# A block's attention units taken from tiles 0 and 3 in turn, then from tiles 1 and 2, and six products without use left out

## The reference

```python
def causal_attention(q, k, v):
    def one_block(args):          # a block is Q_BLOCK = 128 queries
        qb, bi = args
        scores = jnp.einsum('bqhd,bkhd->bhqk', qb, k) * scale
        q_pos = bi * Q_BLOCK + jnp.arange(Q_BLOCK)
        scores = jnp.where(k_pos[None, :] <= q_pos[:, None], scores, -jnp.inf)
        probs = jax.nn.softmax(scores, axis=-1).astype(v.dtype)
        return jnp.einsum('bhqk,bkhd->bqhd', probs, v)
...
    o = causal_attention(q, k, v)
    return rms_norm(o.reshape(b, s, MLA_OUT), out_g)
```

## Time and profile before

| | us |
|---|---|
| median of 3 runs | 2030.34 |
| lowest, highest | 2025.52, 2040.3 |
| the profiled execution's own time | 2028.29 |
| its span | 2026.7 |
| busy in it: PE, DVE, ACT, POOL | 1886.3, 1577.2, 1214.2, 449.5 |
| the block's first product on PE, the next block's | 579.13, 644.42 |

### The profile page before, as it was taken

One profiled execution on the slowest core, in us unless ns is written; L12 is line 12 of the kernel. 1 busy time (PEld: TensorE's weight loads), 2 busy tenths in 40 slices (PEclk: granted clock), 3 DMA queues, 4 the chain that ended last, 5 costly groups with the idle time before them and its releaser, 6 DMA issues.

```text
span 2026.7 us, 27081 instructions
## 1 busy us (share of the span) xinstructions
PE 1886.3 (93%) x9331; PEld 1503.6 (74%) x9331; DVE 1577.2 (78%) x1614; ACT 1214.2 (60%) x1246; POOL 449.5 (22%) x381
## 2 busy tenths in 40 slices
PE   7989988787999886899999999999999999999997
PEld 5766655675767674788888888888888888888884
DVE  4763353674456566889999999999999999999996
ACT  5544564423455322257777777777777777777773
POOL 3435543001034242061311111111111111111110
PEclk9999998998999898799999999999999999999998
DMA  7535441505101105499999999999999999999994
GB/s 201 165 101 190 135 141 44 184 9 134 54 1 28 26 2 179 160 305 348 398 389 398 390 398 389 398 388 390 392 388 394 386 393 381 396 388 394 389 370 148
DMA packets 180401, 525.06 MB, mean 259 GB/s; under 512 B 34530, under 2 KB 52018, under 8 KB 180338
## 3 DMA queue, kind: packets, MB, share of 16 engines
q1 hardware_dynamic: 156882, 458.27, 59.7%
q0 software_dynamic: 21376, 65.95, 11.2%
q10 hardware_dynamic: 2080, 0.01, 0.1%
HBM read 499.06 MB, written 25.12 MB: 259 GB/s over the span
## 4 chain that ended last, share of the span: by engine, by line
PE 56%; DVE 2%; issue 0%; POOLq 0%; POOL 0%; DVEq 0%
PE banks L3354 52%; PE banks L3342 3%; PE banks L3348 1%; PE banks L3418 0%; DVE expert_weights L3692 0%; DVE x_tokens L3688 0%; DVE weights_lo L3488 0%; DVE x_tokens L3699 0%; DVE x_tokens L3571 0%; PE banks L3475 0%; PE banks L3439 0%; PE banks L3409 0%; DVE u_lo L3524 0%; DVE rows_lo L3518 0%; DVE member L3551 0%
## 5 line engine op out<-in xcount | busy, mean ns | idle before, releaser
L3488 DVE TENSOR_TENSOR weights_lo<-expert_weights,weights_hi 128x2048 fp32r<-128x2048 f32 x384 | 877.0, 2288 | 67.3 <-ACT weights_hi L3728 64.2
L3728 ACT ACTIVATE weights_hi<-expert_weights 128x2048 fp32r<-128x2048 f32 x384 | 738.8, 1926 | 266.6 <-PE banks L3354 260.0
L3354 PE MATMUL banks<-weights_hi,rows_hi 128*128 128x512 f32 x1024 | 319.6, 393 | 0.0
L3354 PE MATMUL banks<-weights_hi,rows_lo 128*128 128x512 f32 x1024 | 315.9, 390 | 0.0
L3354 PE MATMUL banks<-weights_lo,rows_hi 128*128 128x512 f32 x1024 | 274.6, 390 | 0.0
L3354 PEld LDWEIGHTS banks<-weights_hi,rows_hi 128*128 128x128 f32 x1024 | 190.0, 188 | 45.1 <-issue 7.3
L3354 PEld LDWEIGHTS banks<-weights_hi,rows_lo 128*128 128x128 f32 x1024 | 192.5, 188 | 40.6
L3354 PEld LDWEIGHTS banks<-weights_lo,rows_hi 128*128 128x128 f32 x1024 | 192.8, 188 | 40.2
L3354 PE MATMUL banks<-weights_hi,u_hi 128*128 128x512 f32 x512 | 161.3, 396 | 1.4 <-DVE u_lo L3524 1.4
L3354 PE MATMUL banks<-weights_hi,u_lo 128*128 128x512 f32 x512 | 158.7, 391 | 0.0
L3354 PE MATMUL banks<-weights_lo,u_hi 128*128 128x512 f32 x512 | 137.5, 390 | 0.0
(11 more groups left out here) (592 smaller groups left out, 2756.6 us busy)
## 6 DMA issues: line engine op xcount, KB each, us to landing
expert_weights<-in_exp_w SPq DMA_DIRECT2D x384, 1024.0 KB, 9.4
enter_rows<-in_ada_w POOLq DMA_DIRECT2D x24, 1024.0 KB, 5.7
w_in_landing<-in_w_in SPq DMA_DIRECT2D x16, 384.0 KB, 3.2
second_landing<-in_w_in SPq DMA_DIRECT2D x12, 512.0 KB, 3.6
x_tokens<-in_x SPq DMA_DIRECT2D x8, 512.0 KB, 6.5
w_in_landing<-in_w_in SPq DMA_DIRECT2D x8, 512.0 KB, 3.7
enter_w_landing<-in_w_out SPq DMA_DIRECT2D x8, 512.0 KB, 5.3
leave_w_landing<-in_w_o SPq DMA_DIRECT2D x8, 512.0 KB, 10.0
```

The lines of the kernel that those rows point to most:

```text
L3354: last = nc.tensor.matmul(c.banks[:, bank + n, :], left[:, 2 * q + kk, :], right[:, q, kk * FF + n * 512:kk * FF + (n + 1) * 512], start=s ...
L3488: nc.vector.tensor_tensor(w_lo[:, ch % SPLIT, :], c.raw[:, ch % RAW if place is None else place, :], w_hi[:, ch % SPLIT, :], ALU.subtract) ...
L3728: nc.scalar.activation(w_hi[:, ch % SPLIT, :], c.raw[:, ch % RAW if place is None else place, :], ACT.Copy).then_inc(hi_ready.sem, 1)
```

## The change

The order of the tiles becomes `PAIRED = (0, TT - 1, 1, 2)`, that is 0, 3, 1, 2. Units 0 to 15 go through the heads and take tile 0 and tile 3 of each; units 16 to 31 do so with tiles 1 and 2. `place_of(i)` gives the place of a unit's tile in the order (0 or 1 in the first half, 2 or 3 in the second), which picks the output bank and the columns of the sums; `units_until(g)` gives the number of units after which the tile at place g is complete: 15, 16, 31, 32. The takes of the first two places stand after `hide` of units 19 and 20, the other two after the loop (before: after units 11, 19 and 27, and at the end). The six products without use inside the loop are gone; those behind it stay. The last tile is now tile 2, so the next block squares the rows of that one. The side work keeps its unit numbers.

```diff
+PAIRED = (0, TT - 1, 1, 2)
...
-    order = tuple(range(TT))
-    units = [(h, t) for t in order for h in range(NH)]
+    order = PAIRED
+    units = [(h, t) for pair in (order[0:2], order[2:4]) for h in range(NH) for t in pair]
+    place_of = lambda i: 2 * (i // (2 * NH)) + i % 2
+    units_until = lambda g: 2 * NH * (g // 2 + 1) - 1 + g % 2
...
-                    g = i // NH
+                    g = place_of(i)
                     if h == 0 and g >= 2:
 
                         pe.wait_ge(taken.sem, g - 1)
...
                     if i in (6, 7):
                         spread_inverses(i - 4)
-                    elif i < 10:
-                        nc.tensor.matmul(c.banks[:, 5, 0:256], c.ident[:], v_tok[:, 0, 0:256], start=True, stop=True)
...
-                                         accum_out=total[:, i:i + 1]).then_inc(probs.sem, 1)
+                                         accum_out=total[:, place_of(i) * NH + units[i][0]:place_of(i) * NH + units[i][0] + 1]).then_inc(probs.sem, 1)
...
-                    dve.wait_ge(probs.sem, (g + 1) * NH)
+                    dve.wait_ge(probs.sem, units_until(g))
...
-                    dve.wait_ge(out_ready.sem, (g + 1) * NH)
+                    dve.wait_ge(out_ready.sem, units_until(g))
...
-                    if i >= 11 and i % NH == 3:
-                        take(i // NH - 1)
+                    if i in (19, 20):
+                        take(i - 19)
+                take(TT - 2)
                 take(TT - 1)
...
-                last_rows = latent["rows"](TT - 1)
+                last_rows = latent["rows"](PAIRED[-1])
...
-                                                          accum_out=latent["sums"][:, TT - 1:TT]))
+                                                          accum_out=latent["sums"][:, PAIRED[-1]:PAIRED[-1] + 1]))
```

## The result

| | before | after |
|---|---|---|
| median of 20 runs each | 2030.42 | 2040.63 |
| lowest, highest | 2025.52, 2040.3 | 2033.01, 2046.43 |
| the profiled execution's own time, its span | 2028.29, 2026.7 | 2035.01, 2033.4 |
| the block's first product, the next block's | 579.13, 644.42 | 581.32, 654.88 |
| the block | 65.29 | 73.56 |

The account below looks back on a forecast made before the run. VectorE was taken to bound the block's start and middle, TensorE its end. Order -0.8 and clock +1.6 made +0.8 us on the median 2030.34, so 2031.1 us, range 2024 to 2037.

Parts of the forecast that it names:

- What bounds the kernel: In the block the change touches first, VectorE sets the start and middle, TensorE the end.
- the start: Up to TensorE's iteration 8: wide units delay unit 4 to 592.2, and TensorE reaches iteration 8 at 597.0.
- the middle: VectorE's masks and side work to the second take: 14.3 us plus 0.9 for waits, ending at 620.2.
- The end: TensorE's work after the second take: 191 steps, 20.9 us, plus 0.3 for the last copy; last output at 641.4.
- the order's term: Whole block: the new tile order alone moves the last output from 642.2 to 641.4, a gain of 0.8 us.
- The clock: Two TensorE stands in the middle, 2.8 and 1.9 us, halve its pace for 3.4 us at the end's beginning: +1.6.
- the one on the other side: At the end the clock stays down, 13 us as from 301 to 314: +5.7, to 2036.0 us; chance 0.13.
- the rival of 6.4 us gained: TensorE never waits in the middle, takes come in time: 2023.9 us; chance 0.12.
- that of +3: The middle is 2 to 3 us longer on VectorE, from last exponents or GpSimd contention: 2033.5 us; chance 0.10.
- The range: Whole time from 2024 to 2037 us, holding all cases, the upper end widened by one.

Follow-up runs that it names:

- fill_both: Changed kernel plus unused 512-column products where TensorE stood, three before unit 16's outputs and two before unit 17's: block 66.05 us.
- fill_bonus_early: fill_both with the copies of the head sums one iteration earlier: block 65.08 us.
- fill_second: Changed kernel plus two unused 512-column products in TensorE's second stand only, before unit 17's outputs: block 67.49 us.
- wake_dense: Changed kernel plus three unused 512-column products in TensorE's iteration 22, after the clock's fall: block 70.92 us.
- wake_thin: Changed kernel plus thirteen unused 64-column products in TensorE's iteration 22, after the clock's fall: block 78.02 us.
- fill_first: Changed kernel plus three unused 512-column products in TensorE's first stand only, before unit 16's outputs: block 71.05 us.
- takes_early: Changed kernel with the two middle takes moved to units 18 and 19, bonus products and scaled rates two units later: block 70.73 us.
- early_fill: Changed kernel with takes at units 18 and 19, scaled rates spread out, head-sum copies earlier, unused 256-column products before units 16 and 17's outputs: block 63.34 us.
- before_no_idle: Kernel before the change with only its six unused products inside the loop removed: block 66.58 us.

## Why the prediction was wrong, point by point

- **What bounds the kernel, the start, the middle**: right, with their numbers. PE came to iteration 8 at 598.9, 17.6 us into the block (17.9 foreseen); mask 14 and the second take within 0.1. Within the middle two misses cancelled: the four decay products took 4.8 instead of 4.5 us and the three bonus products 3.9 instead of 3.6, and of the 0.9 added for ScalarE's exponents only 0.16 shows as a wait. The stands were 2.66 and 1.80 where 2.8 and 1.9 were foreseen. In the start PE stood 1.25 for an inverse and 0.72 before unit 5's scores, not 1.3 there, and the clock held.
- **The end**: the order's term was -0.8 and measured +0.76 at full clock (fill_both). 0.97 of the 1.56 between them is head sums that wait for the copy of the ones before: the sum priced their products and did not look at what releases them. fill_bonus_early shows it. For the other 0.6 there are readings without a run: the fill ended 0.2 behind the take, a head sum takes 0.94 to 1.0 us (638.37 to 639.31, 641.19 to 642.19) where eight steps are 0.88, and the last units, which have no scores beside them, take 3.6 us (649.06 to 652.65) for 28 steps priced at 3.1 and the 0.3 of the last copy.
- **The clock**: this step failed. That the clock would fall about the second stand was foreseen, and it fell at 621. What was mis-sized is how long it stays down: 3.4 us by the mean clock of another place, for 1.6 us of loss. It stayed down 17.1, and cost 7.5 (73.56 less 66.05). I took the shorter of two cases seen elsewhere because "dense work" was to follow. The work that follows keeps PE busy, but with outputs of 64 columns and transposes and scores in ones and twos. The runs show that a PE busy in the profile's sense was not enough: behind the same first stand (2.65 to 2.70 us) the clock stays down 3.4 us (fill_second), 6.8 (wake_dense), 17.1 (after) or 20.5 (wake_thin), by what comes then.
- **The rivals**: what happened is the one on the other side, "the clock falls and stays down", by its mechanism and at its place. It had a chance of 0.13 and a price of +5.7: 6.5 for 13 us at the low level, less the 0.8 of the order. Both terms were too low, 7.5 for 17 us and +0.8 of the order, together the +8.27 of the block. PE did wait in the middle, which rules out the rival of 6.4 us gained; the middle was not longer, which rules out that of +3.
- **The rule cited**: from the Trainium skill ("TensorE: Matmul & The Clock Gate", "Part 1: The HAM clock gate"), which ties the half clock to an idle array and the full one to sustained work, the prediction read that two stands broken by work might leave the clock alone. The traces speak against that: a single stand of 1.87 us was followed by the fall (fill_first), and PE busy in all of 14 us did not end it (takes_early).
- **The range**: its upper end came from a low stretch of 13 us read elsewhere, and one us on top. The trace of before had longer ones, which the prediction did not look at: 17.1 us in the very next block and 20.5 us further on, both with long waits of PE in them. Of these, windows:

```profile
684.00:700.00 16.00, 10.44 (x35) 7.95 (x35) 10.83 (x32) 2.02 (x4) 3.96 (x4) 0.50 0.10 36
841.00:861.00 20.00, 12.44 (x55) 11.64 (x56) 15.60 (x49) 7.58 (x14) 0.93 (x7) 0.50 0.74 265
```

  By the prediction's own way of counting they give 2038.0 and 2039.8. The block's own rows give a wider bound: all of the end's 20.9 us of work at half pace would cost as much again. Two sums of the prediction are off by 0.1 or 0.2, without weight: the gain of the rival without waits is 6.5 and not 6.4, and 2030.34 + 3 is 2033.3 and not 2033.5.

## What to carry to other kernels

The price of a stand of TensorE is more than its own length; it is also what the clock makes of the work behind it: here two stands of 4.5 us together cost 7.5 us by the clock, on top of the wait. Where a wait can't be removed, count the work that follows it twice for the upper bound, as far as nothing is known to bring the clock back; a few products without use inside the wait took that loss away here (five of 512 columns the whole of it, two alone 6.1 us: 73.56 to 67.49). When an order is changed, look also at what releases the small side work in it.

## What was not expected of the hardware

**The clock held in one block, lost in the next.** In fill_both and fill_bonus_early, the next block (`rwkv_core`) took 123.3 and 124.2 us instead of 120.9, and in early_fill 120.9. Windows of it before, and of fill_both:

```profile
644.40:765.30 120.90, 96.44 (x1040) 82.11 (x1041) 81.59 (x180) 39.22 (x83) 39.80 (x35) 0.89 0.10 23
```

```profile
650.00:773.30 123.30, 102.10 (x1040) 87.77 (x1041) 81.61 (x180) 39.23 (x83) 39.81 (x35) 0.85 0.09 23
```

The same 1040 matmuls keep PE busy 5.7 us longer, at a mean clock of 0.85 instead of 0.89: 37 instead of 27 us at the low level. So in these two kernels part of what the clock gained in the block, 2.4 and 3.3 us, was given back in the next one; in early_fill, where the clock held as well, nothing was. Why it is down for longer there was not tried and stays open.

**A square that takes twice as long.** In takes_early and early_fill the squares of the two takes in the middle take 1.55 to 1.71 us on DVE, in before, after and fill_both those of all takes 0.70 to 0.83; one in before_no_idle takes 1.30. One of takes_early, on DVE's timeline:

```profile
615.73 1.71 DVE L2439 CUSTOM_DVE_ANT_0 banks<-h_mix 128x512 f32<-128x512 f32 x1
```

The instruction and its operands are the same; only its place and its neighbours on the engines differ. The two squares cost takes_early 1.6 us more than those of after, and stand ahead of the outputs that PE waits for, so that they are part of why its stands did not shrink as foreseen. No run looked for the cause, and it is open.
